# Down projection as seven block products in 16 groups of 256 ff columns, with part of the sums on GpSimd, and the FFN norm applied ahead of the up projection

## What is computed

```
def rmsnorm(x, w):
    y = xf * lax.rsqrt(jnp.mean(xf * xf, axis=-1, keepdims=True) + NORM_EPS)
    return y * w
...
    h = h + jnp.concatenate([conv_out, ret_out], axis=-1) @ w_out
    f = jnp.square(jax.nn.relu(rmsnorm(h, norm_ffn_w) @ w_up)) @ w_down
    return h + f
...
y_prompt = rmsnorm(hp[:, N_META:], norm_final_w)
y_sample = rmsnorm(hs, norm_final_w)
```

## Time and profile before

| | |
|---|---|
| median of 3 runs | 1288.22 us (1287.36 to 1289.46) |
| profiled execution: span, first to last instruction | 1285.8 us |
| median less that span | 2.4 us |
| PE busy | 1267.7 us (99% of the span) |
| DVE, ACT, POOL busy | 593.1, 328.1, 0.2 us |

### The profile page before, as it was taken

One profiled execution on the slowest core, in us unless ns is written; L12 is line 12 of the kernel. 1 busy time (PEld: TensorE's weight loads), 2 busy tenths in 40 slices (PEclk: granted clock), 3 DMA queues, 4 the chain that ended last, 5 costly groups with the idle time before them and its releaser, 6 DMA issues.

```text
span 1285.8 us, 17987 instructions
## 1 busy us (share of the span) xinstructions
PE 1267.7 (99%) x6972; PEld 1170.4 (91%) x6972; DVE 593.1 (46%) x1171; ACT 328.1 (26%) x647; POOL 0.2 (0%) x4
## 2 busy tenths in 40 slices
PE   8999999999999899999999999999999999999997
PEld 6999999999999688998998998998998998988986
DVE  7545444454456454642443443443443443443446
ACT  6332232232233211330330330330320320420433
POOL 0000000000000000000000000000000000000000
PEclk9999999999999899999999999999999999999999
DMA  6111111111112710120120120220220210220203
GB/s 227 46 38 46 42 38 46 41 37 45 41 37 82 217 46 1 49 83 1 49 83 1 49 81 0 64 66 0 65 65 0 71 59 0 82 65 0 82 33 106
DMA packets 88339, 70.20 MB, mean 55 GB/s; under 512 B 9440, under 2 KB 73056, under 8 KB 88304
## 3 DMA queue, kind: packets, MB, share of 16 engines
q1 hardware_dynamic: 88304, 69.73, 18.1%
HBM read 64.73 MB, written 4.99 MB: 54 GB/s over the span
## 4 chain that ended last, share of the span: by engine, by line
PE 95%; DVE 2%; DMA 1%; issue 1%; ACT 1%; DVEq 0%; SPq 0%; ACTq 0%
PE ps L1047 29%; PE ps L1049 29%; PE ps L1048 29%; PE ps L1054 1%; PE ps L1053 1%; DMA normw<-in_norm_ffn_w 1%; PE ps L1223 1%; PE ps L1146 1%; PE ps L1164 1%; PE ps L1163 1%; PE ps L1153 1%; PE ps L1132 1%; PE ps L1064 1%; DVE wo_lo L876 0%; DMA raw<-in_w_out 0%
## 5 line engine op out<-in xcount | busy, mean ns | idle before, releaser
L1047 PE MATMUL ps<-mid_hi,ws_hi 128*128 128x368 f32 (+1 forms) x768 | 251.3, 327 | 0.2 <-DVE ws_lo L955 0.2
L1049 PE MATMUL ps<-mid_hi,ws_lo 128*128 128x368 f32 (+1 forms) x768 | 251.4, 327 | 0.0
L1048 PE MATMUL ps<-mid_lo,ws_hi 128*128 128x368 f32 (+1 forms) x768 | 250.8, 327 | 0.0
L1047 PE MATMUL ps<-hn_hi,ws_hi 128*128 128x368 f32 (+1 forms) x648 | 219.7, 339 | 1.2 <-DVE hn_lo L724 1.2
L1048 PE MATMUL ps<-hn_lo,ws_hi 128*128 128x368 f32 (+1 forms) x648 | 213.3, 329 | 0.0
L1049 PE MATMUL ps<-hn_hi,ws_lo 128*128 128x368 f32 (+1 forms) x648 | 212.8, 328 | 0.0
L981 DVE SCALAR_TENSOR_TENSOR h<-ps,inv_ms,h 128x512 f32<-128x512 f32 (+1 forms) x144 | 108.0, 750 | 226.7 <-PE ps L1049 217.2
L1047 PE MATMUL ps<-wd_hi,f_hi 128*128 128x512 f32 x512 | 199.2, 389 | 0.0
L1048 PE MATMUL ps<-wd_lo,f_hi 128*128 128x512 f32 x512 | 199.2, 389 | 0.0
L1049 PE MATMUL ps<-wd_hi,f_lo 128*128 128x512 f32 x512 | 199.2, 389 | 0.0
L624 ACT ACTIVATE wd_hi<-raw 128x512 fp32r<-128x512 f32 x64 | 39.3, 625 | 438.8 <-PE ps L1049 438.8
(11 more groups left out here) (162 smaller groups left out, 1263.0 us busy)
## 6 DMA issues: line engine op xcount, KB each, us to landing
raw<-in_w_up SPq DMA_DIRECT2D x64, 256.0 KB, 3.0
raw<-in_w_down SPq DMA_DIRECT2D x64, 256.0 KB, 2.8
raw<-in_w_in SPq DMA_DIRECT2D x56, 256.0 KB, 2.9
raw<-in_w_out SPq DMA_DIRECT2D x16, 256.0 KB, 3.0
out<-hw SPq DMA_DIRECT2D x16, 256.0 KB, 2.0
xr<-in_x_prompt SPq DMA_DIRECT2D x7, 512.0 KB, 6.2
h<-in_x_prompt SPq DMA_DIRECT2D x1, 3072.0 KB, 19.7
h<-in_x_prompt SPq DMA_DIRECT2D x1, 1024.0 KB, 7.4
```

Of the source, the lines that this page charges most:

```text
L1047: pe.matmul(out, a_hi, b_hi, start=start, stop=False)
L1048: pe.matmul(out, a_hi, b_lo, start=False, stop=False)
L1049: return pe.matmul(out, a_lo, b_hi, start=False, stop=stop)
```

## The change

**Down projection.** There are 16 groups of 256 ff columns. The group's product of f (1024 tokens x 256) with w_down (256 x 1024) is cut in 2 x 2 blocks, 512 tokens x 128 by 128 x 512, and is formed with seven block products in place of eight (Winograd's form): `P1`..`P7`, each of four token tiles `q` and three matmuls of 512 columns. That needs sums of blocks of w_down (`T1`..`T4`, all on GpSimd), sums of blocks of f (`S1`, `S2` on DVE, `S3`, `S4` on GpSimd), hi and lo parts of all seven operands on either side, and sums of the products: some are left to accumulate in a PSUM bank, 16 results a group are added to `h` by DVE (`add`), and 12 are copied from PSUM by ACT (`copy_out`, four buffers `tmp`) and added to `h` by GpSimd. The sample tokens keep the plain product. w_down comes through four slots `dr` that share their place with `hw`.

**Norm.** ACT sums squares of `h` (`rms`), DVE applies divisor and weight in one instruction (`normed_ffn`), `inverse_ms` is gone, and the additions need no factor. The transpositions stand later in PE's program.

```diff
-GROUPS = 8
-FT = FF // GROUPS // P
+GROUPS = 16
+QUADS = 4
...
+STAGES = [(p, q) for p in range(OPS) for q in range(QUADS)]
+ORDER = [*STAGES, "sample"]
...
+            def load_down(g, first):
+                if first:
+                    sp.wait_ge(ht_done, TILES)
                 else:
...
+                    sp.wait_ge(d_ready, len(D_LO) * g)
+                for k in range(2):
+                    for nh in range(2):
...
+                        sp.dma_start(dr[:, k, nh, :], src).then_inc(dr_in[2 * k + nh], 16)
...
+            def copy_out(g, k, last):
+                p, q = (POOL_ADDS_LAST if last else POOL_ADDS)[k]
+                act.wait_ge(prod_done, NPROD * g + n_prod(p, q, last))
+                act.wait_ge(pool_add, NPOOL * g + k + 1)
+                act.activation(tmp(k, last), bank_of(p, q)[:, :], ACT.Copy).then_inc(act_copy, 1)
...
+                base = NU * HEADS + 2 * g
+                act.wait_ge(prod_done, NPROD * g + 1)
+                for name in D_LO:
+                    d_hi(g, name)
+                act.wait_ge(w_used, base + 1)
+                split_ffn(g, "up", 1, 0)
...
+                for k in range(len(POOL_ADDS_LAST if last else POOL_ADDS)):
+                    copy_out(g, k, last)
+                if last:
+                    for p in range(5):
+                        final_early(p)
+                        final_late(p)
...
+            def d_low(g, name):
+                dve.wait_ge(d_hi_ready, len(D_LO) * g + D_LO.index(name) + 1)
+                if name in ("T1", "T2"):
+                    dve.wait_ge(d_sum, 4 * g + 4)
...
+                add(g, P1, 0, last)
+                f_low(g, "A12")
...
+                pool.wait_ge(prod_done, NPROD * g + 1)
+                for n in range(4):
+                    pool.wait_ge(dr_in[n], 16 * g + 16)
...
+                pool.tensor_tensor(t1, b12, b11, ALU.subtract).then_inc(d_sum, 1)
+                pool.tensor_tensor(t3, b22, b12, ALU.subtract).then_inc(d_sum, 1)
+                pool.wait_ge(d_sum, 4 * g + 1)
+                pool.tensor_tensor(t2, b22, t1, ALU.subtract).then_inc(d_sum, 1)
+                pool.wait_ge(d_sum, 4 * g + 3)
+                pool.tensor_tensor(t4, b21, t2, ALU.subtract).then_inc(d_sum, 1)
...
+                for k, (p, q) in enumerate(adds):
+                    pool.wait_ge(act_copy, NPOOL * g + k + 1)
...
+                    pool.tensor_tensor(h_part(p, q), tmp(k, last), h_part(p, q), ALU.add).then_inc(pool_add, 1)
...
+            pool.wait_ge(ht_ready, TILES)
...
+                elif p == P6:
+                    pe.wait_ge(dve_add, NDVE * g + n_dve_add(P1, q, last_group))
...
+                elif p == P4:
+                    pe.wait_ge(dve_add, NDVE * g + n_dve_add(P7, q, last_group))
...
+                passes(bank_of(p, q)[:, :], fo_hi[:, p, at:at + P], fo_lo[:, p, at:at + P], do_hi[:, p, :], do_lo[:, p, :],
+                       start=p in FRESH, stop=True, again=p not in FRESH).then_inc(prod_done, 1)
```

More of the change, by code:

```diff
@@ L632, in _ @@
                     split_ffn(0, "up", 0, 1)
-            rl_flat = rl[:, :, :].rearrange("p s c -> p (s c)")[:, 0:512]
-            def group(g, last):
[L637 to L653, removed]
+                if 1 <= t < TILES - 1:
+                    rms(t + 1)
@@ L968, in _ @@
                     split_ffn(0, "up", 0, 1)
[L969 to L989 removed]
+                residual(t)
@@ L1023, in group @@
+                for name in D_LO:
+                    d_low(g, name)
+                split_ffn(g, "up", 1, 0)
+                f_low(g, "A11")
+                split_ffn(g, "up", 1, 1)
+                f_low(g, "f1")
+                f_low(g, "S3")
                 if not last:
                     split_ffn(g, "next", 0, 0)
-                    split_ffn(g, "next", 0, 1)
-                for p in range(TILES):
-                    take_down(g, p, last)
-                    if last and p >= 1:
-                        final_norm(p - 1)
@@ new lines, in group @@
+                dve.tensor_tensor(f12[:, :], fr[:, 0, SEQ:TY], fr[:, 1, SEQ:TY], ALU.add).then_inc(f_sum_dve, 1)
+                add(g, P1, 0, last)
+                f_low(g, "A12")
+                add(g, P1, 1, last)
+                f_low(g, "S2")
+                add(g, P1, 2, last)
+                add(g, P1, 3, last)
+                f_low(g, "f12")
+                f_low(g, "S1")
+                for q in range(QUADS):
+                    add(g, P2, q, last)
+                f_low(g, "A22")
@@ new lines, in group @@
+                if not last:
+                    split_ffn(g, "next", 0, 1)
+                f_low(g, "S4")
+                if not last:
+                    for p, q in DVE_ADDS[8:]:
+                        add(g, p, q, False)
+                    sample_add(g, False)
+                    return
+                for p, q in DVE_ADDS_LAST[8:12]:
+                    add(g, p, q, True)
+                add(g, P5, 2, True)
+                add(g, P5, 3, True)
+                dve.wait_ge(normw_in, 32)
@@ L1034, in _ @@
+                final_norm(0)
+                final_norm(1)
+                sample_add(g, True)
+                add(g, P7, 2, True)
+                add(g, P7, 3, True)
+                final_norm(2)
+                add(g, P3, 2, True)
+                add(g, P3, 3, True)
+                final_norm(3)
+                add(g, P4, 2, True)
+                add(g, P4, 3, True)
+                for p in range(4, TILES):
+                    final_norm(p)
             with dve.Fori(0, GROUPS - 1) as g:
-                chain["base"] = g * 2
```

504 lines of the change are left out of this document (343 added, 161 removed).

## The result

| | before | after |
|---|---|---|
| median, us | 1287.79 (1285.35 to 1289.46, 4 runs) | 1337.37 (1336.59 to 1343.35, 4 runs) |
| ratio | | 1.0399, 95% interval 1.0376 to 1.0423 |
| profiled execution: time, span, us | 1288.2, 1285.8 | 1337.05, 1335.3 |
| mean granted clock | 0.995 | 0.985 |

What follows compares the result with a forecast made beforehand. PE, busy 99% of the span, was taken to bound the kernel, so only the count of matmuls matters. 1288.2 - 43.5 (fewer matmuls) + 4 (loop) + 11.6 (first group) + 13.8 (last group) = 1274 us; range 1256 to 1330.

Steps and rivals of the forecast that it cites:

- the first rival: In groups, POOL and DVE instructions with two SBUF operands exclude each other: 4.6 us each, 69 in all, 1339 us; chance 0.30.
- 192 matmuls fewer: Down projection: 1344 matmuls of 512 columns in place of 1536, at 0.227 us each, -43.5 us.
- loop through POOL: Before each second up block, POOL's chain takes 18.7 us against 18.44: PE waits 0.25, in 15 groups +4 us.
- first group: Late sample transposition, load of `dr` and POOL's sums delay the second up block, then half clock: together +11.6 us.
- last group: Final norms ahead of `P7`'s additions hold `P4`'s third tile and leave DVE in arrears: +13.8 us in all.
- the covered waits of `A12` and `P4`: Steady groups: `A12`'s low part ready 0.1 us before `P2`, `P7`'s addition at 36.2 before `P4` at 37.3; cost nothing.
- The Trainium skill's rule: Cited for the exclusion: a DVE instruction with two SBUF inputs contends with a GpSimd one reading SBUF; the loser blocks.
- POOL's price: One POOL addition of 512 columns taken at 1.2 us, range 0.6 to 1.6, without a row in the trace.
- ACT and DVE with room as a sum: Per 44.6 us group, DVE's work sums to 26 us and ACT's to 23: no bound.
- the out projection at nothing: Out projection: ACT's `rms` and DVE's `normed_ffn` fall within 10.9 us of PE work per tile, costing nothing.

Runs made afterwards that it cites:

- with the collisions taken away: Changed kernel with the early split, two added GpSimd waits where it would collide, and P3 added by VectorE straight from PSUM: 1273.18 us, ratio 0.988.
- the version with the last group's order: Changed kernel with the additions of P7, tiles 2 and 3, ahead of final norms 0 and 1 and the sample's additions in the last group: 1332.22 us.
- the version with GpSimd's two waits: On the early split, GpSimd waits for VectorE before sum S4 and before its additions of P6: 1283.08 us, ratio 0.9975.
- the early split: Changed kernel with the weight split of the second up block's first half ahead of T1 to T4's copies and low parts: 1301.47 us, ratio 1.0107.

## Why the prediction was wrong

The forecast was 1274 us and faster; measured were 1337, and the time of the first rival was 1339. The working by its own steps, in us:

| step | forecast | first rival | measured |
|---|---|---|---|
| 192 matmuls fewer | -43.5 | the same | -43.5, and +0.2 in each of 16 groups, +3.2 |
| `P2` and `P4`, 15 groups | 0 | 2.8 each, 42 | 1.89 each, 28 |
| loop through POOL, 15 groups | 0.25 each, 4 | 1.8 each, 27 | 1.98 each, 30 |
| first group | 11.6 | the same | 14.4 |
| last group | 13.8 | the same | 19.0 |

The measured column adds up to 1288.2 + 51 = 1339.4 against a profiled 1337.05; the 2 us over are open. That the rival's sum came so near is luck in part: it has `P2` and `P4` 14 us too dear and both edges 8 too cheap.

**The step that failed** is the covered waits of `A12` and `P4`: "Nothing for these" was 28 us. Next to it the loop's 0.25 a group, which was 1.98, 26 us more; there the mechanism was right and the size wrong. I had the right objection in the text and gave it 0.30, "no row here has them at work together" being my reason against. That is no reason: POOL was idle in the trace, which speaks for neither side. The Trainium skill's rule stood beside it and was the only evidence there was; the runs bear it out.

**The size of it.** The products take 21.15 us in the changed kernel and 19.26 with the collisions taken away, 1.89 a group, where I had 2.8 for the rival. By the starts `P2` lost 0.6, near the rival's 0.5 (`A12`'s low part takes 1.32 and not 0.69). `P4` lost 1.2 and not 2.3: between 713.36 and 717.8 three of DVE's instructions took 1.09, 1.77 and 1.79 us, 2.6 too many, where the rival had up to 3.6, and DVE had 1.1 to spare.

**The loop.** By the rows, 1.98 is made of my 0.25, of 12 x (1.26 - 1.2) = 0.7 for POOL's price, and of the holding of `T1`, `T3`, `T2`, 1.65 + 1.74 + 1.74 - 3 x 1.29 = 1.3; less 0.4, since POOL begins `P4`'s additions 6.18 us ahead of the up projection (721.46 to 727.64) and not 5.77. Together 1.85. No run separates the terms: each run that took away the one changed another. POOL's price was a good choice, near the upper row of 1.225; but the place had no room at all, and "each 0.1 us of POOL's price is 1.2 us a group" made even a miss of 0.06 worth 11 us. The rival had the holding at 1.95.

**The first group.** From the transposition to the second block are 544.52 - 528.91 = 15.6 us, not 14.1. The block comes 544.52 - 520.69 = 23.8 us after the group's first matmul instead of 11.87, 12.0 late, and then runs at half clock (granted 0.50 to 549.74):

```profile
544.98 0.49 PE L1305 MATMUL ps<-mid_lo,ws_hi 128*128 128x352 f32 x1
545.27 0.49 PE L1306 MATMUL ps<-mid_hi,ws_lo 128*128 128x352 f32 x1
...
549.74 0.39 PE L1306 MATMUL ps<-mid_hi,ws_lo 128*128 128x368 f32 x1
549.97 0.33 PE L1304 MATMUL ps<-mid_hi,ws_hi 128*128 128x368 f32 x1
550.13 0.33 PE L1305 MATMUL ps<-mid_lo,ws_hi 128*128 128x368 f32 x1
```

Starts are 0.29 apart, later 0.16: the first 17 take 549.74 - 544.52 = 5.22 us, where 17 x 0.165 are 2.8, so 2.4 too many. 14.4 in all; the mechanism was right.

**The last group.** From its start (1276.77 - 11.87) to the end of the span are 70.4 us, where I had 65.2. What the trace has beyond my working: half clock behind the wait at its second up block (granted 0.50, some 1.5 us by the 16.74 from there to `P2`, where the version with the last group's order has 15.19); earlier waits of PE of 0.29 and 1.61 us, where I had 0.7, with DVE's low parts of 0.88 and 1.77 us ahead of the second; the first final norm beside POOL's last additions, 2.88 us instead of 1.41; PE's last six matmuls at half clock (granted 0.50), behind a wait of 4.93; and VectorE's waits of 0.83 and 1.18 us for the stores to free `hw`, which I had not looked for. How the 5.2 are shared among them is not shown:

```profile
1309.59 2.88 DVE L1204 SCALAR_TENSOR_TENSOR hw<-h,fin,normw 128x512 f32<-128x512 f32 x2
1327.21 1.41 DVE L1204 SCALAR_TENSOR_TENSOR hw<-h,fin,normw 128x512 f32<-128x512 f32 x2 [0.83 <-DMA out<-hw]
```

**What was right**: the 192 matmuls and their price; POOL's price to 5%; ACT and DVE with room as a sum; the out projection at nothing; the signs at both edges, with sizes 2.8 of 14.4 and 5.2 of 19.0 us short. The change with its collisions taken away and four additions a group moved gives 1273 us, by chance the forecast's number: it has the edges dearer and the loop free.

## What to carry to other kernels

An engine that is idle in the trace says nothing on what it collides with: before work is moved to GpSimd, mark every VectorE instruction with two SBUF operands that can lie beside it, and either order the two by a semaphore or give GpSimd only gaps. What counts is not GpSimd's busy share (30% here) but its unbroken runs: beside one, a low part of VectorE mostly took 1.6 to 1.85 us, and 7.27 or more in the places where it was passed over. And a chain that closes with 0.25 us missing in a loop should be priced as a wait, with the cheapest way to shorten it (here four additions a group moved back to VectorE, 31 us) noted beside it.

## What the hardware showed that I had not expected

- Beside a stream of GpSimd additions a VectorE instruction with two SBUF operands mostly gets its turn after one of them (1.58 to 1.85 us for one of 0.69, 31 of 34), but it can be passed over: 166.08 and 5.33 us in that run, 7.27 to 7.46 in each group of the version with GpSimd's two waits, and at one place of the early split 2.35 us in ten groups and 6.2 in five. It also turns round: three low parts in a row held one GpSimd addition for 2 us.
- GpSimd memsets (0.46 us from start to start at 512 columns) cost VectorE nothing: 691 ns beside them. Even an addition of 4 columns is held by VectorE's low parts, 1.36 us instead of 0.2.
- A VectorE addition with one operand in PSUM took 679 ns in the mean beside GpSimd, and 683 where GpSimd only wrote.
- After PE's idle times of 9.39 and 4.93 us the matmuls ran at half clock (granted 0.50), for 5.2 us in the first case and to the end of PE's work in the second (the last starts are 0.43 us apart). After a wait of 2.13 us they did so in five groups of one run and not in the others.
